# Neighbourhood attention: where the stacks of a head's second half and the second turn of V stand in the order of work

## The chip, the cores and the metric

The kernel runs on one core of a Trainium2 chip. The metric is the device time of one execution in microseconds (us); less is better. TensorE (PE) does the matrix products and the transposes, VectorE (DVE), ScalarE (ACT) and GpSimd (POOL) the element-wise work. Each engine works through its own list of instructions in order and waits at semaphores for the others.

## The reference, cut to what matters

Two post-LayerNorm layers on 1024 tokens of width 1024. The first mixes tokens by differential attention, the second, which the change is in, by attention over a neighbourhood of 8 rows by 16 columns on a grid of 16 rows by 64 columns. A gated feed-forward block with a short convolution follows each.

```python
def neighborhood_attention(x, w_qkv, b_qkv, rpb, w_o, b_o):
    qkv = x @ w_qkv + b_qkv                    # 16 heads of width 64
    ...
    def row(r):
        r_start = jnp.clip(r - kh // 2, 0, rows - kh)
        ...
        s = jnp.einsum('bchd,bicjhd->bhcij', q_row, k_sel)
        bias = rpb[:, row_off[None, :, None], col_off[:, None, :]]
        p = jax.nn.softmax((s + bias[None]).reshape(B, H, GRID_W, kh * kw), axis=-1)
        return jnp.einsum('bhcij,bicjhd->bchd', p, v_sel)
    ...
    return o @ w_o + b_o
```

## The kernel before

All matrix products are made in pieces: a float32 operand is split into a high part and the low remainder, and the products of high and low parts are added up in PSUM. Only `neighbourhood_stage` matters here. It takes the 16 heads in 8 pairs; a pair is `h` in the code and is called a head in this text. Each head has 16 steps `s`: steps 0 to 7 are the eight query tiles of its first half (`c` = 0), steps 8 to 15 those of its second half (`c` = 1). There are thus 128 steps, and the Python loops are unrolled: every engine has one long list, whose order is written out by hand.

In step `s` of head `h` the engines do this:

- **TensorE**: `score(h, s)` (into one of three PSUM banks), `turn` (four transposes of the probabilities of two steps back, into one of two banks `tb`), `weigh` (probabilities times V of four steps back, into `pb`), and then a chunk of the projection of the next head, `project(h + 1, j, ...)`. The six projection pieces `j` = 0 to 5 (two each for Q, K and V) have 24 matrix products each; `CHUNKS` deals them out as 12 in each of steps 0 to 3 and 8 in each later step. All six use the one PSUM bank `pa`, so that the first product of a piece waits until ScalarE has taken the piece before it out of `pa`.
- **VectorE**: adds the bias to the scores and takes the minimum (line 1841), makes the low part of the turned probabilities (`low`, line 1792), inverts the sum (line 1851), and every second step sums the output (`add_o`, lines 1806 and 1813).
- **ScalarE**: `high` (line 1725, the high part of the turned probabilities), the exponential (line 1770), `take_o` every second step (line 1740), and, where `TAKE` or the head's first line says so, `take(h, j)` (line 1716), which moves a finished projection piece from `pa` to `raw`.
- **GpSimd**: scales the probabilities (line 1516), splits weights, and builds the bias tables.

Each half of a head needs its **stacks**: the high parts of K and Q (`stacks` on ScalarE, lines 1748 and 1749), then the low parts and a copy (`stacks` on VectorE, lines 1819, 1822 and 1825), and a copy and the padded queries on GpSimd (`double_k`, `pad_q`). Steps 8 and on of the head need the stacks of the second half. They read `raw`, and `take(h + 1, 0)` in step 2, which overwrites `raw`, waits until VectorE has finished `stacks(h, 1)`'s reads:

```python
                        if TAKE[s] == 0:
                            act.wait_ge(stack_low[1], 2 * h + 2)
```

V of the head is turned in step 3 by `turn_v(h, 0)` and `turn_v(h, 1)`, four transposes each, into the same two banks `tb` that `turn` uses; each waits for the `low` that empties its bank. ScalarE's `high_v` (line 1732) and VectorE's `low_v` (line 1798) take the two halves out. The first `weigh` of the head, `weigh(h, 0)` in step 4, waits for both:

```python
                if s == 0:
                    pe.wait_ge(t_low, v_index(h, 1) + 1)
```

The list of ScalarE begins each head with `take(h, 5)`, the last piece of that head's own V; the first chunk of the next head's projection, in step 0, waits for it.

Of the kernel before, what the change touches and what calls it, by code (L numbers as in the profile page):

```python
# [1341 lines left out]
def neighbourhood_stage(nc, w_qkv, b_qkv, Z, OT, XTh, XTl, ident, S, GW, KH_, KW, shared_raw, next_tiles):  # L1342
# [3 lines left out]
    H = D // P  # L1346
# [20 lines left out]
    with ExitStack() as ctx:  # L1367
# [47 lines left out]
        def bank(h, j):  # L1415

            return pb[0] if h == 0 and j % 2 else pa

        def t_index(h, s):

            return TURNS * h + (s if s < 2 else s + 2)
# [9 lines left out]
        def back(h, s, n):  # L1431

            return (h, s - n) if s >= n else (h - 1, s - n + STEPS)
# [154 lines left out]
        def _(pe):  # L1588
# [92 lines left out]
            for h in range(H):  # L1681
                done = 0
                for s in range(STEPS):
                    score(h, s)
                    if h or s >= 2:
                        turn(*back(h, s, 2))
                    if h or s >= 4:
                        weigh(*back(h, s, 4))
                    if s == 3:
                        turn_v(h, 0)  # L1690
                        turn_v(h, 1)
                    if h + 1 < H:
                        project(h + 1, done // (3 * KT), done % (3 * KT), CHUNKS[s])
                        done += CHUNKS[s]
            for s in range(4):
                if s < 2:
                    turn(*back(H, s, 2))
                weigh(*back(H, s, 4))

        @block.scalar  # L1700
        def _(act):
            nc.scalar.preload_act_table(ACT.Exp)
            for j in range(3):

                if j == 2:
                    act.wait_ge(w_in[0], 16)
                nc.scalar.activation(wh[:, j], wraw[:, j % 2], ACT.Copy).then_inc(w_high, 1)
            act.wait_ge(b_turned, 1)
            nc.scalar.activation(bq[:].rearrange("p j h -> p (j h)"), pb[1][:, 0:3 * H], ACT.Copy).then_inc(b_set, 1)
            act.wait_ge(b_set, 1)  # L1710
            nc.scalar.activation(bq[:, 0], bq[:, 0], ACT.Copy, scale=-(DH ** -0.5)).then_inc(b_scaled, 1)
            act.wait_ge(b_scaled, 1)

            def take(h, j):
                act.wait_ge(proj_done, 6 * h + j + 1)
                nc.scalar.activation(raw[:, j // 2, (j % 2) * BANK:(j % 2 + 1) * BANK], bank(h, j)[:], ACT.Identity,  # L1716
                                     bias=bq[:, j // 2, h:h + 1],
                                     scale=-(DH ** -0.5) if j < 2 else 1.0).then_inc(proj_out, 1)

            def high(h, s):  # L1720
                step, i = STEPS * h + s, t_index(h, s)
                act.wait_ge(turned, i + 1)
                if step >= 3:
                    act.wait_ge(pv_done, step - 2)
                nc.scalar.activation(PT[:, step % 3, :, 0], tb[i % 2][:], ACT.Copy).then_inc(t_high, 1)

            def high_v(h, part):
                i = v_index(h, part)
                act.wait_ge(turned, i + 1)
                if h and part == 0:  # L1730
                    act.wait_ge(pv_done, STEPS * h)
                nc.scalar.activation(V[:, part * KB:(part + 1) * KB, :, 0],
                                     tb[i % 2][:].rearrange("p k (c d) -> p k c d", c=2), ACT.Copy).then_inc(t_high, 1)

            def take_o(h, s):
                pair = 8 * h + s // 2
                act.wait_ge(pv_done, STEPS * h + s + 1)
                if pair:
                    act.wait_ge(o_out, pair)
                nc.scalar.activation(otmp[:], pb[pair % 2][DH:P, :], ACT.Copy).then_inc(o_half, 1)  # L1740

            def stacks(h, c):
                a, _ = halves(c)
                if c == 0:
                    act.wait_ge(proj_out, 6 * h + 4)
                if h:
                    act.wait_ge(scored, STEPS * h - QT * (1 - c))
                nc.scalar.activation(KH[a, c], raw[a, 1], ACT.Copy).then_inc(stack_high[c], 1)
                nc.scalar.activation(QS[a, c], raw[a, 0], ACT.Copy).then_inc(stack_high[c], 1)

            for j in range(4):
                take(0, j)
            stacks(0, 0)
            take(0, 4)
            for h in range(H):
                take(h, 5)
                for s in range(STEPS):
                    step = STEPS * h + s
                    if s in TAKE and h + 1 < H:
                        if TAKE[s] == 0:  # L1760
                            act.wait_ge(stack_low[1], 2 * h + 2)
                        if TAKE[s] == 4:
                            act.wait_ge(turned, v_index(h, 1) + 1)
                        take(h + 1, TAKE[s])
                    if step >= 2:
                        high(*back(h, s, 2))
                    act.wait_ge(biased, step + 1)
                    if step >= 4:
                        act.wait_ge(turned, t_index(*back(h, s, 4)) + 1)
                    nc.scalar.activation(E[:, s % 4], Sc[step % 3][:], ACT.Exp, scale=-1.0, bias=mn[:, s % 4:s % 4 + 1],  # L1770
                                         accum_out=den[:, s % 4:s % 4 + 1]).then_inc(exped, 1)
                    if s % 2 and step >= 4:
                        take_o(*back(h, s, 4))
                    if s == 0:
                        stacks(h, 1)
                    if s == 3:
                        high_v(h, 0)
                        high_v(h, 1)
                    if s == 11 and h + 1 < H:
                        stacks(h + 1, 0)  # L1780
            for s in range(4):
                if s < 2:
                    high(*back(H, s, 2))
                if s % 2:
                    take_o(*back(H, s, 4))

        @block.vector
        def _(dve):
# [43 lines left out]
            for h in range(H):  # L1832
                for s in range(STEPS):
                    c, qt = s // QT, s % QT
# [3 lines left out]
                    if qt == 0:  # L1838
# [3 lines left out]
                                                   in1=bias.rearrange("p r k -> p (r k)"), scale=1.0, scalar=3.0e38,  # L1842
                                                   op0=ALU.add, op1=ALU.min,
                                                   accum_out=mn[:, s % 4:s % 4 + 1]).then_inc(biased, 1)
                    if step >= 2:
                        low(*back(h, s, 2))
                    if s == 3:
                        low_v(h, 0)
                        low_v(h, 1)
                    dve.wait_ge(exped, step + 1)  # L1850
                    nc.vector.reciprocal(rden[:, s % 4:s % 4 + 1], den[:, s % 4:s % 4 + 1]).then_inc(inverted, 1)  # L1851
                    if s % 2 and step >= 4:
                        add_o(*back(h, s, 4))
                    if s == 1:
                        stacks(h, 1)
                    if s == 12 and h + 1 < H:
                        stacks(h + 1, 0)
# [62 lines left out]
```

## Time and profile before

| | before |
|---|---|
| median of 3 runs | 2976.95 us (2975.7 to 2981.74) |
| profiled execution | 2978.02 us |
| its span in the profile | 2976.2 us |
| TensorE busy | 2764.6 us, 93% of the span |
| VectorE busy | 1801.3 us, 61% |
| ScalarE busy | 895.8 us, 30% |
| GpSimd busy | 1250.8 us, 42% |
| mean granted clock of TensorE | 0.974 of full speed |
| neighbourhood stage | about 1556 to 2102 us of the span |

The profiled execution lasted 1.82 us longer than its span and 1.07 us longer than the median. A share of busy time is a mean over stages. In the rows further down a number in square brackets behind an instruction is the time for which its engine sat idle right before it, and behind the arrow stands what ended that idle time.

### The profile page before, as it was taken

Reading aid. Unit: us, or ns where it says so; the run is one execution under the profiler, and the core shown is the slowest. Engines: PE = TensorE matmul, PEld = TensorE weight load, DVE = VectorE, ACT = ScalarE, POOL = GpSimd, SP = SyncE. Lnnn points to the kernel's source line nnn. Section 1 sums busy time; section 2 is a strip of 40 time slices with the busy share of each in tenths; the row PEclk is TensorE's granted clock in tenths of the full one; section 3 lists DMA queues with packets and bytes.
Section 4 is the critical chain, followed back from the end, with each engine's and each line's share of the span. In section 5 each row is a group of like instructions: output and inputs, shape, how many; then the busy total and the mean of one; then the engine's idle time right before and its main releaser. Section 6 shows DMA issues by size and latency. Waiting matters only on the chain. (4 is left out here: it accounts for less than half of the span.)

```text
span 2976.2 us, 36581 instructions
## 1 busy us (share of the span) xinstructions
PE 2764.6 (93%) x13387; PEld 2302.9 (77%) x13387; DVE 1801.3 (61%) x2190; ACT 895.8 (30%) x1314; POOL 1250.8 (42%) x890
## 2 busy tenths in 40 slices
PE   7999999968899999999979999998789999999998
PEld 6788888756778888887867887787667888888886
DVE  3666766654484555555573677767467554555557
ACT  3455445542311111111133555455322111111111
POOL 2444444233563333333444555555366333333335
PEclk9999999988999999999989999999899999999999
DMA  3000002215111111111121212111601111111111
GB/s 115 26 29 28 23 26 51 56 50 185 51 36 57 49 42 49 49 42 49 50 79 45 56 47 49 41 43 22 210 26 62 43 43 50 53 44 49 44 48 71
DMA packets 212649, 163.16 MB, mean 55 GB/s; under 512 B 34939, under 2 KB 194251, under 8 KB 212555
## 3 DMA queue, kind: packets, MB, share of 16 engines
q1 hardware_dynamic: 212411, 161.38, 18.4%
q8 instruction: 59, 0.97, 0.1%
q10 hardware_dynamic: 144, 0.52, 0.0%
q14 instruction: 35, 0.29, 0.0%
HBM read 137.24 MB, written 24.64 MB: 54 GB/s over the span
## 5 line engine op out<-in xcount | busy, mean ns | idle before, releaser
L1129 PE MATMUL ff_ph<-XTh,WH 128*128 128x512 f32 x1408 | 550.1, 391 | 6.8 <-PEq L41 6.8
L1129 PE MATMUL ff_ph<-XTl,WH 128*128 128x512 f32 x1408 | 549.3, 390 | 0.0
L1129 PE MATMUL ff_ph<-XTh,WL 128*128 128x512 f32 x1408 | 549.2, 390 | 0.0
L1067 POOL TENSOR_SCALAR WH<-raw_weights 128x1024 fp32r<-128x1024 f32 x128 | 153.5, 1200 | 846.6 <-PE ff_ph L1129 471.9
L1277 DVE TENSOR_SCALAR ff_C<-ff_H,ff_par 128x1024 f32<-128x1024 f32 x88 | 199.3, 2265 | 430.2 <-ACT ff_H L1225 429.5
L1069 POOL TENSOR_TENSOR WL<-raw_weights,WH 128x1024 fp32r<-128x1024 f32 x128 | 340.2, 2658 | 10.7
L1129 PEld LDWEIGHTS ff_ph<-XTh,WH 128*128 128x128 f32 x1408 | 265.4, 188 | 62.7 <-issue 7.6
L1129 PEld LDWEIGHTS ff_ph<-XTh,WL 128*128 128x128 f32 x1408 | 265.3, 188 | 55.4
L1129 PEld LDWEIGHTS ff_ph<-XTl,WH 128*128 128x128 f32 x1408 | 265.4, 189 | 55.1
L1225 ACT ACTIVATE ff_H<-ff_ph,ff_par 128x1024 f32<-128x1024 f32 x88 | 98.3, 1117 | 571.0 <-PE ff_ph L1129 571.0
L1270 DVE TENSOR_TENSOR X<-ff_po,X 128x512 f32<-128x512 f32 x288 | 192.1, 686 | 103.5 <-PE ff_po L1143 103.5
L1143 PE MATMUL ff_po<-WH 128*128 128x512 f32 x576 | 228.7, 397 | 23.0 <-DVE X L1270 20.7
L1143 PE MATMUL ff_po<-WL,WH 128*128 128x512 f32 x576 | 225.0, 391 | 0.0
L1143 PE MATMUL ff_po<-WH,WL 128*128 128x512 f32 x576 | 225.0, 391 | 0.0
L547 ACT ACTIVATE da_E<-da_S,da_mn 128x1024 f32<-128x1024 f32 x128 | 142.9, 1117 | 226.5 <-DVE da_mn L660 223.7
L1516 POOL TENSOR_SCALAR na_E<-na_E,na_rden 128x512 f32<-128x512 f32 x128 | 96.3, 753 | 213.3 <-DVE na_rden L1851 213.2
L1279 DVE SCALAR_TENSOR_TENSOR ff_C<-ff_H,ff_par,ff_C 128x1024 f32<-128x1024 f32 x88 | 168.9, 1919 | 11.0 <-DVE ff_C L1277 0.3
L1602 PE MATMUL na_pa<-XTh,na_wh 128*128 128x512 f32 x360 | 145.3, 404 | 28.9 <-ACT na_raw L1716 22.0
L347 PE MATMUL da_pa<-XTh,da_wh 128*128 128x512 f32 x360 | 151.5, 421 | 10.0 <-POOL da_wl L272 3.8
L278 POOL TENSOR_SCALAR da_E<-da_E,da_rden,da_neglam 128x1024 f32<-128x1024 f32 x64 | 76.6, 1197 | 199.8 <-DVE da_rden L674 199.8
L660 DVE CUSTOM_DVE_ANT_0 da_S<-da_S,da_strip 128x1024 f32<-128x1024 f32 x128 | 153.8, 1241 | 9.2 <-PE da_S L361 8.2
L1143 PEld LDWEIGHTS ff_po<-WH 128*128 128x128 f32 x576 | 108.4, 188 | 59.6 <-DVE X L1270 38.2
(222 smaller groups left out, 5952.0 us busy)
## 6 DMA issues: line engine op xcount, KB each, us to landing
raw_weights<-in_ffn_w_in SPq DMA_DIRECT2D x88, 512.0 KB, 3.8
raw_weights<-in_ffn_w_out SPq DMA_DIRECT2D x44, 512.0 KB, 3.5
raw_weights<-in_attn_w_qkv SPq DMA_DIRECT2D x24, 512.0 KB
raw_weights<-in_na_w_qkv SPq DMA_DIRECT2D x24, 512.0 KB, 4.2
wo_oraw<-heads_t SPq DMA_DIRECT2D x16, 512.0 KB, 4.7
rpb_rows<-da_rows SPq DMA_DIRECT2D x2, 3840.0 KB, 26.5
na_B<-rpb_rows SPq DMA_DIRECT2D x32, 224.0 KB, 4.2
da_E<-in_x SPq DMA_DIRECT2D x8, 512.0 KB, 5.7
```

Of the source, the lines that this page charges most:

```text
L347: last = nc.tensor.matmul(out[:], w[:, j // 2, k], x[:, k, t0:t0 + BANK], start=(i == 0), stop=(i == 3 * KT - 1))
L547: nc.scalar.activation(E[:, t % 2, c], Sc[c][:], ACT.Exp, scale=-1.0, bias=mn[:, t % 2, c:c + 1], accum_out=den[:, t % 2, c:c + 1]).then_i ...
L660: nc.vector.tensor_tensor_reduce(out=Sc[c][:], in0=Sc[c][:], in1=strip[:, (QT - 1 - t) * P:(QT - 1 - t) * P + S], scale=1.0, scalar=3.0e38 ...
L1067: nc.gpsimd.tensor_scalar(wh[:, slot], wraw[:, raw_slot], 1.0, 1.0, ALU.mult, ALU.mult).then_inc(w_high, 1)
L1069: nc.gpsimd.tensor_tensor(out=wl[:, slot], in0=wraw[:, raw_slot], in1=wh[:, slot].bitcast(F32), op=ALU.subtract).then_inc(w_low, 1)
L1129: last = nc.tensor.matmul(out[:, at], wt[:, slot, k * P:(k + 1) * P], x[:, k, at], start=(k == 0 and n == 0), stop=(k == KT - 1 and n == 2))
L1143: last = nc.tensor.matmul(po[r % 4][:], a[:, f, t * P:(t + 1) * P], wt[:, slots[f], half * BANK:(half + 1) * BANK], start=(f == 0 and n == ...
L1225: nc.scalar.activation(H[:, parity, 1:S + 1], ph[parity][:].rearrange("p k n -> p (k n)"), ACT.Identity, bias=par[:, 0, bass.ds(idx, 1)]). ...
L1270: nc.vector.tensor_tensor(out=at, in0=po[r % 4][:], in1=at, op=ALU.add).then_inc(added, 1)
L1277: nc.vector.tensor_scalar(c, h[:, 1:S + 1], tap[2], tap[4], ALU.mult, ALU.add).then_inc(conv_link, 1)
L1279: nc.vector.scalar_tensor_tensor(out=c, in0=h[:, 0:S], scalar=tap[1], in1=c, op0=ALU.mult, op1=ALU.add).then_inc(conv_link, 1)
L1602: last = nc.tensor.matmul(out[:], w[:, j // 2, k], x[:, k, t0:t0 + BANK], start=(i == 0), stop=(i == 3 * KT - 1))
```

## The change

Three edits of order; no instruction is added or removed, and what each computes is the same.

```diff
--- before.py
+++ after.py
@@ TensorE, step loop
                     if s == 3:
                         turn_v(h, 0)
-                        turn_v(h, 1)
                     if h + 1 < H:
                         project(h + 1, done // (3 * KT), done % (3 * KT), CHUNKS[s])
                         done += CHUNKS[s]
+                    if s == 3:
+                        turn_v(h, 1)
@@ ScalarE
-            stacks(0, 0)
+            for c in range(2):
+                stacks(0, c)
             take(0, 4)
             for h in range(H):
                 take(h, 5)
@@ ScalarE, step loop, behind take(h + 1, TAKE[s])
+                    if s == 4:
+                        high_v(h, 1)
                     if step >= 2:
                         high(*back(h, s, 2))
...
-                    if s == 0:
-                        stacks(h, 1)
                     if s == 3:
                         high_v(h, 0)
-                        high_v(h, 1)
                     if s == 11 and h + 1 < H:
                         stacks(h + 1, 0)
+                    if s == 15 and h + 1 < H:
+                        stacks(h + 1, 1)
@@ VectorE, step loop, behind the bias addition
+                    if s == 4:
+                        low_v(h, 1)
                     if step >= 2:
                         low(*back(h, s, 2))
                     if s == 3:
                         low_v(h, 0)
-                        low_v(h, 1)
...
-                    if s == 1:
+                    if s == 0:
                         stacks(h, 1)
```

**ScalarE, from step 15 of one head into step 2 of the next.** `na_E` is the exponential, `na_otmp` is `take_o`, `na_raw` is `take`, `na_PT` is `high`, and `na_KH` and `na_QS` are the stacks. Before:

```order
L1770 ACTIVATE na_E,na_den<-na_S,na_mn 128x512
L1740 ACTIVATE na_otmp<-na_pb 64x512
L1716 ACTIVATE na_raw<-na_pa,na_bq 128x512
L1725 ACTIVATE na_PT<-na_tb 128x4x128
L1770 ACTIVATE na_E,na_den<-na_S,na_mn 128x512
L1748 ACTIVATE na_KH<-na_raw 64x1024
L1749 ACTIVATE na_QS<-na_raw 64x1024
L1725 ACTIVATE na_PT<-na_tb 128x4x128
L1770 ACTIVATE na_E,na_den<-na_S,na_mn 128x512
L1740 ACTIVATE na_otmp<-na_pb 64x512
L1716 ACTIVATE na_raw<-na_pa,na_bq 128x512
```

The same stretch of the changed kernel, whose lines are numbered a little higher:

```order
L1774 ACTIVATE na_E,na_den<-na_S,na_mn 128x512
L1741 ACTIVATE na_otmp<-na_pb 64x512
L1749 ACTIVATE na_KH<-na_raw 64x1024
L1750 ACTIVATE na_QS<-na_raw 64x1024
L1717 ACTIVATE na_raw<-na_pa,na_bq 128x512
L1726 ACTIVATE na_PT<-na_tb 128x4x128
L1774 ACTIVATE na_E,na_den<-na_S,na_mn 128x512
L1726 ACTIVATE na_PT<-na_tb 128x4x128
L1774 ACTIVATE na_E,na_den<-na_S,na_mn 128x512
L1741 ACTIVATE na_otmp<-na_pb 64x512
L1717 ACTIVATE na_raw<-na_pa,na_bq 128x512
```

The two stacks have moved ahead of `take(h, 5)`, the first `na_raw`, and no longer stand between the exponential of step 0 and the `na_PT` of step 1.

**VectorE, step 4.** The bias addition is listed as two `ISA` rows, `na_PT` is `low`, `na_V` is `low_v`, `na_rden` the inversion. Before:

```order
L1813 TENSOR_TENSOR na_ostage<-na_osum 64x256
L1841 ISA na_S,na_mn<-na_S,na_BI 128x512
L1841 ISA na_mn 128x1
L1792 TENSOR_TENSOR na_PT<-na_tb,na_PT 128x4x128
L1851 RECIPROCAL na_rden<-na_den 128x1
```

The same stretch of the changed kernel:

```order
L1816 TENSOR_TENSOR na_ostage<-na_osum 64x256
L1844 ISA na_S,na_mn<-na_S,na_BI 128x512
L1844 ISA na_mn 128x1
L1801 TENSOR_TENSOR na_V<-na_tb,na_V 128x8x64
L1795 TENSOR_TENSOR na_PT<-na_tb,na_PT 128x4x128
L1855 RECIPROCAL na_rden<-na_den 128x1
```

V's second half now stands behind the bias addition of step 4, which itself waits for that step's scores.

**TensorE, the end of step 3 and step 4 up to the `weigh` that waits for V.** `na_pa` is the last product of step 3's chunk, `na_S` are the scores, `na_tb<-ident,na_E` is `turn`, `na_pb` is `weigh`, and `na_tb<-ident,na_raw` is `turn_v`. Before:

```order
L1602 MATMUL na_pa<-XTh,na_wl 128x512
L1622 MATMUL na_S<-na_KH,na_QS 128x448
L1623 MATMUL na_S<-na_KL,na_QS 128x448
L1628 MATMUL na_S<-na_KH,na_QZ 128x64
L1629 MATMUL na_S<-na_KL,na_QZ 128x64
L1628 MATMUL na_S<-na_KH,na_QZ 128x64
L1629 MATMUL na_S<-na_KL,na_QZ 128x64
L1638 MATMUL na_tb<-ident,na_E 128x128 x4
L1666 MATMUL na_pb<-na_PT,na_V 128x256 x4
```

The same stretch of the changed kernel:

```order
L1602 MATMUL na_pa<-XTh,na_wl 128x512
L1648 MATMUL na_tb<-ident,na_raw 128x128 x4
L1622 MATMUL na_S<-na_KH,na_QS 128x448
L1623 MATMUL na_S<-na_KL,na_QS 128x448
L1628 MATMUL na_S<-na_KH,na_QZ 128x64
L1629 MATMUL na_S<-na_KL,na_QZ 128x64
L1628 MATMUL na_S<-na_KH,na_QZ 128x64
L1629 MATMUL na_S<-na_KL,na_QZ 128x64
L1638 MATMUL na_tb<-ident,na_E 128x128 x4
L1666 MATMUL na_pb<-na_PT,na_V 128x256 x4
```

Before, the second four transposes of V stood with the first four, ahead of the twelve products of step 3; now only the scores and one `turn` lie between them and the `weigh` that needs their result. The lists of GpSimd and of the DMA queue are unchanged.

## Rows read from the trace of the kernel before

**Rows 1.** Who waited for whom on TensorE, 1556 to 2100 us (total, times, longest)
```profile
PE na_pa L1602 <- ACT na_raw L1716: 22.0, 14, 2.5
PE na_tb L1638 <- POOL na_E L1516: 13.0, 14, 2.2
PE na_tb L1648 <- DVE na_PT L1792: 9.3, 9, 4.8
```

**Rows 2.** Stretches: length, busy PE, PEld, DVE, ACT, POOL, granted clock, DMA
```profile
1595.00:1604.00 9.00, 7.77 (x38) 6.14 (x36) 4.79 (x9) 4.23 (x8) 3.50 (x3) 1.00 0.01 3
1604.00:1610.00 6.00, 5.33 (x19) 4.34 (x20) 2.81 (x5) 1.89 (x4) 2.43 (x3) 0.72 0.00 0
1722.00:1787.00 65.00, 60.84 (x354) 52.30 (x352) 45.98 (x89) 34.52 (x69) 35.76 (x37) 1.00 0.20 48
```

**Rows 3.** Timeline of ScalarE, end of the second head, start of the third
```profile
1723.22 0.60 ACT L1740 ACTIVATE na_otmp<-na_pb 64x512 f32<-64x512 f32 x1
1723.85 0.69 ACT L1716 ACTIVATE na_raw<-na_pa,na_bq 128x512 f32<-128x512 f32 x1
...
1726.17 0.69 ACT L1770 ACTIVATE na_E<-na_S,na_mn 128x512 f32<-128x512 f32 x1 [1.15 <-DVE na_mn L1841]
...
1726.97 1.05 ACT L1748 ACTIVATE na_KH<-na_raw 64x1024 fp32r<-64x1024 f32 x1
...
1729.00 0.60 ACT L1725 ACTIVATE na_PT<-na_tb 128x512 fp32r<-128x512 f32 x1
...
1735.33 0.69 ACT L1716 ACTIVATE na_raw<-na_pa,na_bq 128x512 f32<-128x512 f32 x1 [4.30 <-DVE na_QS L1822]
```

**Rows 4.** Timeline of TensorE, steps 0 to 4 of that head
```profile
1724.68 0.47 PE L1602 MATMUL na_pa<-XTh,na_wh 128*128 128x512 f32 x1 [0.91 <-ACT na_raw L1716]
...
1731.76 0.36 PE L1622 MATMUL na_S<-na_KH,na_QS 128*128 128x448 f32 x1
...
1736.07 0.50 PE L1602 MATMUL na_pa<-XTh,na_wh 128*128 128x512 f32 x1 [2.41 <-ACT na_raw L1716]
...
1740.68 0.60 PE L1648 MATMUL na_tb<-ident,na_raw 128*128 128x128 f32 x4
1741.78 0.66 PE L1648 MATMUL na_tb<-ident,na_raw 128*128 128x128 f32 x4 [0.50 <-DVE na_PT L1792]
1742.20 0.47 PE L1602 MATMUL na_pa<-XTh,na_wh 128*128 128x512 f32 x1
...
1745.05 0.36 PE L1622 MATMUL na_S<-na_KH,na_QS 128*128 128x448 f32 x1
...
1746.22 0.72 PE L1666 MATMUL na_pb<-na_PT,na_V 128*128 128x256 f32 x4
1746.78 0.39 PE L1602 MATMUL na_pa<-XTh,na_wh 128*128 128x512 f32 x1
```

**Rows 5.** Timeline of VectorE, steps 0 to 4 of that head
```profile
1726.98 0.16 DVE L1851 RECIPROCAL na_rden<-na_den 128x1 f32<-128x1 f32 x1 [0.30 <-ACT na_E L1770]
...
1732.82 1.22 DVE L1819 TENSOR_TENSOR na_KL<-na_raw,na_KH 64x1024 fp32r<-64x1024 f32 x1
...
1735.93 0.70 DVE L1841 CUSTOM_DVE_ANT_0 na_S<-na_S,na_BI 128x512 f32<-128x512 f32 x1
...
1736.55 0.69 DVE L1792 TENSOR_TENSOR na_PT<-na_tb,na_PT 128x512 fp32r<-128x512 f32 x1
...
1746.02 0.70 DVE L1841 CUSTOM_DVE_ANT_0 na_S<-na_S,na_BI 128x512 f32<-128x512 f32 x1 [0.65 <-PE na_S L1629]
```

**Rows 6.** Timeline of the first head, steps 1 to 3: VectorE, then TensorE
```profile
1601.04 1.22 DVE L1819 TENSOR_TENSOR na_KL<-na_raw,na_KH 64x1024 fp32r<-64x1024 f32 x1
...
1605.38 0.70 DVE L1841 CUSTOM_DVE_ANT_0 na_S<-na_S,na_BI 128x512 f32<-128x512 f32 x1
...
1604.67 0.50 PE L1602 MATMUL na_pa<-XTh,na_wh 128*128 128x512 f32 x1 [1.48 <-ACT na_raw L1716]
...
1609.11 0.37 PE L1622 MATMUL na_S<-na_KH,na_QS 128*128 128x448 f32 x1
```

## The prediction

> **What bounds the kernel now.** I read first the page's shares: TensorE is busy for 93% of the span, so a change outside the neighbourhood stage's TensorE list can matter only through its waits. The change is in that stage alone, so I asked next who was waited for on TensorE there. ScalarE's `take` costs it 22.0 us in 14 waits, GpSimd's scaling 13.0 us, VectorE's `low` in front of V's second turn 9.3 us [rows 1]. The stretch of one head, 65 us, has TensorE busy for 60.84 us at the full granted clock (1.00, 2.4 GHz), while VectorE, ScalarE and GpSimd are busy for 45.98, 34.52 and 35.76 us [rows 2]. So TensorE is the bound from head to head, and the time moves by what its four waits per head move. The timeline of one head shows them: 0.91 us at step 0 for `take(h, 5)`, 2.41 us at step 2 for `take(h + 1, 0)`, 0.50 us at step 3 for `low(h, 1)` [rows 4]; a fourth, for a scaling, isn't touched. The last head projects nothing and is bound by the smaller engines in turn.
>
> **The wait at step 2** is a chain over VectorE. Its stacks begin at 1732.82, behind the output sum of step 1 [rows 5]; ScalarE's `take(h + 1, 0)` has idled 4.30 us until K's and Q's low parts are made and starts at 1735.33 [rows 3]; TensorE follows at 1736.07 [rows 4]. In the changed kernel the stacks stand two output operations and one step earlier, so this wait should go.
>
> **The price at step 0.** `take(h, 5)` starts at 1723.85 with no idle time before it, right behind `take_o` of 1723.22 (0.60 us) [rows 3]: here ScalarE's own queue is the limit, and TensorE waits for it (0.91 us). The change puts both stacks of ScalarE between the two. They run from 1726.97 until the next instruction starts at 1729.00, 2.03 us [rows 3]. Nothing hides them: the projection can't start before `take` has emptied `pa`. So TensorE's first product of step 0 moves from 1724.68 to 1726.71, and its idle time grows to 2.94 us. That is the term which the change adds, and it is nearly as large as the one it removes.
>
> **Step 2, worked forward.** From the first product of step 0 to the scores of step 2 TensorE needs 1731.76 - 1724.68 = 7.08 us, so these start at 1733.79. From scores with four partial products to the next projection it needs 1746.78 - 1745.05 = 1.73 us [rows 4]; ready for step 2's chunk at 1733.79 + 1.73 = 1735.52. Is `take(h + 1, 0)` done by then? `take(h, 5)` now starts at 1725.88, `high` some 0.6 us later and takes as long, so that the exponential of step 0 starts at about 1727.06; the inversion follows 0.81 us behind it, at 1727.87, as that of 1726.98 [rows 5] follows the exponential of 1726.17 [rows 3]. VectorE's stacks begin at about 1728.05. They take 1735.93 - 1732.82 = 3.11 us in this head [rows 5], but 1605.38 - 1601.04 = 4.34 us in the first, where GpSimd's scaling begins beside them [rows 6]. In the new place it always does. The bias addition of step 1 thus starts at 1731.2 to 1732.4; 0.8 us to its exponential (it takes 0.70 us, and the minimum is read out behind it), 0.8 us through it, 0.6 us for `take_o`, and 0.75 us for `take` give 1734.1 to 1735.3, and never before the previous chunk's end, 1733.8, plus 0.75. All of it lies before 1735.52. So the wait is gone, and the chunk starts 0.55 us before its old time of 1736.07. It holds by 0.2 us at the upper bound.
>
> The Trainium skill (GPSIMD Engine Reference, section 8, Key points) says that GpSimd shares its SBUF interfaces with VectorE and contends with two-input operations. The pair 3.11 and 4.34 us agrees with it; it gives no figure for this pair.
>
> **Step 3.** The first turn of V moves with the chunk: 1740.68 - 0.55 = 1740.13. Before, chunk three began 1742.20 - 1740.68 = 1.52 us behind it; one turn alone passes in 1742.20 - 1741.78 = 0.42 us. The chunk starts at 1740.55, takes 1745.05 - 1742.20 = 2.85 us, the second turn starts at 1743.40, the scores of step 4 at 1743.82 [rows 4]. Two turns now cost 0.84 us instead of 1.52, a gain of 0.68; the idle 0.50 understates it.
>
> **A new wait at step 4.** `weigh(h, 0)` needs `low_v(h, 1)`, and VectorE has this behind the bias addition of step 4, which waits for step 4's scores. That addition starts 1746.02 - 1745.05 = 0.97 us behind the scores' start [rows 4, 5]. The next operation ends 1736.55 + 0.69 - 1735.93 = 1.31 us behind the addition's start [rows 5]. With 0.05 us to TensorE, as from `take`'s end (1736.02) to 1736.07, `weigh` starts at 1743.82 + 0.97 + 1.31 + 0.05 = 1746.15; without the wait it would be 1743.82 + 1.17 = 1744.99. So 1.16 us are lost, where before there was no wait. ScalarE's `high_v(h, 1)` is not late: the turn ends at 1744.06 and `take(h + 1, 1)` lies beside it. Late next behind `low_v` is `low` of step 2, which has until step 6.
>
> **The sum.** Per head +2.03 - 2.58 - 0.68 + 1.16 = -0.07 us: `weigh(h, 0)` at 1746.15 instead of 1746.22. Behind it the list is the old one. Six heads have all four terms (the second to the seventh): -0.4 us. The first has no step-0 term, since its stacks run on ScalarE during the opening projections. Its VectorE stacks start some 3.7 us earlier, and its wait of 1.48 us [rows 6] shrinks to about 0.3, so -1.2; V's two terms are about -1.0 and +1.16. Together -1.0 to -1.4. In the last head nothing is projected: the stacks leave VectorE's step 1 for step 0, the bias addition of step 2 still ends where the same total work ends, and V's two `low_v` change places with an addition; I take +0.3, bounds -0.5 and +1.5. Sum: -0.4 - 1.2 + 0.3 = -1.3 us. From the profiled execution's 2978.02 us (1.82 above its span) that is 2976.7; the median of the runs shown is 1.07 us lower, so 2975.6 us. Within 0.2% (6 us), about what a measurement of this kernel can tell from no change.
>
> **Rivals.** (1) The clock falls in the longer stall: slower. In the first head the granted clock is 0.72 from 1604 to 1610, after a stretch with waits of which the last is 1.48 us [rows 2, 6]: twelve products take 1609.11 - 1604.67 = 4.44 us instead of 2.85, a loss of 1.59. Against it: the third head keeps 1.00 through a wait of 2.41 us [rows 2, 4], and no wait of the later heads for `take` is longer than 2.5 [rows 1]. But 2.94 us is longer than any of these, and the quiet stretch begins with short transposes. The mechanism: step 0's stall lets the clock fall to 1.2 GHz for the chunk behind it, in each of six heads. Price 6 x 1.59 = 9.5, total 2975.6 + 9.5 = 2985.1 us; from five heads on it decides for slower. In one to three heads it gives 2977 to 2980, still no change. The Trainium skill (TensorE: Matmul & The Clock Gate, Part 1) says the clock is gated by how busy the array has lately been, only between half and full rate. The 0.72 is a mixture of these two; by that rule the longer stall is the riskier. (2) The wait at step 2 stays in part, because VectorE's stacks with GpSimd beside them hold up step 1: for 1 us more than my upper bound, +0.8 per head and 2981, for 1.2 us and more slower than by 0.2%, up to 2984. Against it stand the bounds above. (3) The new wait at step 4 doesn't appear, VectorE getting to `low_v` before the bias addition's scores are needed: -1.16 in seven heads, 2967.5. Against it stands the order of VectorE's list. (4) ScalarE's stacks are hidden at step 0, and the change does what its parts promise: six times 2.03 less, 2963. Against it: `take(h, 5)` without idle time.
>
> **How the numbers follow.** My sum within 0.2%: 0.50. Rival 1 in few heads, also no change: 0.14; in five or six: 0.17. Rival 2 beyond 0.2%: 0.06. Rival 3: 0.08; rival 4: 0.03; 0.02 for a last head worse than its bound. Faster 0.11, same 0.64, slower 0.25. An error of 0.4 us per head in the four terms is 2.4 us, with the last head's bounds some 3 us either way; the range reaches down towards rival 3 and up to rival 1: 2970.5 to 2985.5.
>
> **What would show it.** Right: per head a wait of about 2.9 us at step 0 for line 1717, none at step 2, none before either turn of V, and about 0.9 us of idle time before step 4's `weigh`, released by VectorE's `low_v`; head to head 64.85 us instead of 64.92. Wrong: granted clock under 1.00 in the heads' stretches (rival 1), a wait at step 2 for `take` (rival 2), no idle before that `weigh` (rival 3), a step-0 wait still near 0.9 us (rival 4).

## The result, and the profile after

The changed kernel takes 2985.20 us (median of 9 runs, 2983.76 to 2987.50) against 2978.56 us (9 runs, 2975.70 to 2981.74) for the kernel before, timed beside it: a ratio of 1.0023, 95% interval 1.0013 to 1.0033. It is slower by 0.23%. The forecast was 2975.6 us and no change; the first rival, the clock that falls in the longer stall, gave 2985.1 us and slower.

The profiled execution took 2984.45 us, with a span of 2982.6 us against 2976.2 us before. The page of the changed kernel, its span and the busy time of each engine:

```profile
span 2982.6 us, 36581 instructions
PE 2774.4 (93%) x13387; PEld 2310.5 (77%) x13387; DVE 1805.3 (61%) x2190; ACT 893.5 (30%) x1314; POOL 1252.8 (42%) x890
```

This says nothing of the cause yet. The waits on TensorE in the neighbourhood stage do. The view that answers to [rows 1], for the changed kernel (total us, times, longest):

```profile
PE na_pa L1602 <- ACT na_raw L1717: 18.0, 7, 2.9
PE na_tb L1638 <- POOL na_E L1516: 15.7, 15, 3.5
PE na_pb L1666 <- DVE na_V L1801: 7.4, 8, 1.1
...
PE na_tb L1648 <- DVE na_PT L1795: 1.2, 2, 0.7
```

`take` was waited for 14 times, at most 2.5 us; now there are 7 waits, and six of them are of 2.93 to 2.94 us, all at step 0. The nine waits before V's turns are two, and both lie in the last head. A wait for `low_v` (line 1801) is new, eight times. For `take` and V together TensorE waits 18.0 + 7.4 + 1.2 = 26.6 us where it waited 22.0 + 9.3 = 31.3; with the scalings (15.7 instead of 13.0) it is 42.3 instead of 44.3. By its waits the kernel should be a little faster.

What it gave back is in the stretches. Each row below is one head of the changed kernel (the third and the fourth), from one step-0 wait to the next; the columns are those of [rows 2], the granted clock third from the end:

```profile
1719.10:1785.40 66.30, 62.05 (x353) 53.37 (x352) 46.33 (x91) 34.23 (x68) 36.46 (x37) 0.97 0.20 47
1785.40:1852.60 67.20, 63.04 (x352) 54.15 (x352) 46.23 (x91) 34.23 (x68) 36.33 (x37) 0.95 0.19 46
```

TensorE has the 352 products that it had, but is busy for 62 to 63 us with them instead of 60.84 [rows 2], and the granted clock is 0.97 or 0.95 instead of 1.00. The timeline of TensorE for steps 0 to 4 of the third head, which answers to [rows 4], shows where:

```profile
1723.58 0.67 PE L1602 MATMUL na_pa<-XTh,na_wh 128*128 128x512 f32 x1 [2.94 <-ACT na_raw L1717]
1724.05 0.63 PE L1602 MATMUL na_pa<-XTl,na_wh 128*128 128x512 f32 x1
1724.48 0.63 PE L1602 MATMUL na_pa<-XTh,na_wl 128*128 128x512 f32 x1
...
1727.54 0.39 PE L1602 MATMUL na_pa<-XTl,na_wh 128*128 128x512 f32 x1
1727.76 0.39 PE L1602 MATMUL na_pa<-XTh,na_wl 128*128 128x512 f32 x1
1727.99 0.39 PE L1622 MATMUL na_S<-na_KH,na_QS 128*128 128x512 f32 x1
...
1732.21 0.36 PE L1622 MATMUL na_S<-na_KH,na_QS 128*128 128x448 f32 x1
...
1733.95 0.39 PE L1602 MATMUL na_pa<-XTh,na_wh 128*128 128x512 f32 x1
...
1738.43 0.60 PE L1648 MATMUL na_tb<-ident,na_raw 128*128 128x128 f32 x4
1738.79 0.48 PE L1602 MATMUL na_pa<-XTh,na_wh 128*128 128x512 f32 x1
...
1741.63 0.60 PE L1648 MATMUL na_tb<-ident,na_raw 128*128 128x128 f32 x4
1741.99 0.45 PE L1622 MATMUL na_S<-na_KH,na_QS 128*128 128x448 f32 x1
...
1744.41 0.74 PE L1666 MATMUL na_pb<-na_PT,na_V 128*128 128x256 f32 x4 [0.91 <-DVE na_V L1801]
```

Behind the wait of 2.94 us the products follow each other at 0.43 us (1724.05 to 1724.48), at the end of the same chunk at 0.22 us (1727.54 to 1727.76). That is 1.2 and 2.4 GHz. The chunk takes 1727.99 - 1723.58 = 4.41 us. From there to step 4 there is no wait, at step 2 and before either turn of V, and then the 0.91 us before `weigh`.

The lengths of heads in this text are measured on TensorE from the `turn` of one head's step 0 (behind its 0.34 us wait for a scaling) to that of the next; the first head begins with the stage's first product and the last ends with the first product of the next stage. The six later heads (second to seventh) take 399.02 us in the changed kernel and 389.50 before: 66.50 instead of 64.92 us each, +9.52 us. The first head takes 2.99 us less, the last one 2.16 us more. Together +8.69 us for the stage (562.23 instead of 553.54). The rest of the span, which the change doesn't touch, came out 2.3 us shorter in this profile. That is noise of this size: in the eleven profiles of this case the part ahead of the stage alone, which no edit touches, took between 1557.8 and 1562.7 us, and the 9 runs of the kernel before lie 6 us apart. So a single profile's stage and a median agree only to a few microseconds.

### The profile page after: what moved, and what is told of

Its sections match the earlier page's. It is cut to its first block and busy times, and to the rows that moved or that the text cites. A ratio compares the mean times of both kernels' runs of the same rounds, so it can differ in the third digit from the quotient of the medians.

```text
span 2982.6 us, 36581 instructions
## 1 busy us (share of the span) xinstructions
PE 2774.4 (93%) x13387; PEld 2310.5 (77%) x13387; DVE 1805.3 (61%) x2190; ACT 893.5 (30%) x1314; POOL 1252.8 (42%) x890
## 5 line engine op out<-in xcount | busy, mean ns | idle before, releaser
L1516 POOL TENSOR_SCALAR na_E<-na_E,na_rden 128x512 f32<-128x512 f32 x128 | 103.1, 805 | 239.1 <-DVE na_rden L1855 239.1
```

The lines of the kernel that those rows point to most:

```text
L1516: nc.gpsimd.tensor_scalar(E[:, b], E[:, b], rden[:, b:b + 1], 1.0, ALU.mult, ALU.mult).then_inc(scaled, 1)
```

## The experiments

Nine kernels, each timed against the kernel before. The runs were made on three chips (e1_fill, e2_stacks, e3_v and e5_behind on one, e6_best, e7_half, e8_v_fill and e9_bstacks on another, e10_before_fill on a third), so the column "before" shows what the kernel before took beside each, and medians of different chips compare less exactly than their differences from it. Two theories stand against each other. By the first the loss is the clock that falls behind the step-0 wait, and the order alone costs nothing. By the second it is in the order itself, above all in the `weigh` that waits for V, and the clock is only a sign of idle time.

| kernel | median us (runs) | before, us | ratio, 95% interval |
|---|---|---|---|
| e1_fill | 2973.45 (11) | 2979.74 | 0.9979, 0.9970 to 0.9988 |
| e2_stacks | 2980.49 (11) | 2979.74 | 1.0006, 0.9997 to 1.0015 |
| e3_v | 2989.93 (7) | 2979.74 | 1.0034, 1.0022 to 1.0045 |
| e5_behind | 2971.29 (8) | 2979.74 | 0.9972, 0.9961 to 0.9982 |
| e7_half | 2976.81 (11) | 2978.83 | 0.9990, 0.9981 to 0.9999 |
| e8_v_fill | 2982.36 (11) | 2978.83 | 1.0011, 1.0002 to 1.0020 |
| e9_bstacks | 2961.26 (5) | 2978.83 | 0.9941, 0.9928 to 0.9955 |
| e6_best | 2956.27 (5) | 2978.83 | 0.9925, 0.9912 to 0.9939 |
| e10_before_fill | 2976.11 (11) | 2979.49 | 0.9986, 0.9977 to 0.9995 |

**The changed kernel with products in the step-0 wait (e1_fill).** The order of all instructions is that of the changed kernel. In heads two to seven, TensorE does twelve products more while it would wait. They go into a bank of scores that is free then and is overwritten later, so the output is unchanged.

```diff
                     if s == 3:
                         turn_v(h, 0)
+                    if s == 0 and h and h + 1 < H:
+                        pe.wait_ge(exped, STEPS * h - 1)
+                        for i in range(12):
+                            nc.tensor.matmul(Sc[(STEPS * h + 1) % 3][:], wh[:, 2, i % KT], XTh[:, i % KT, 0:BANK],
+                                             start=True, stop=True)
                     if h + 1 < H:
```

> The changed kernel with twelve further matrix products on TensorE in step 0 of the second to seventh head, put between the weigh and the projection, where it otherwise idles 2.94 us for take(h, 5). They write a score bank that the next step overwrites, so the output is unchanged; at the full clock they take some 2.7 us, less than the wait. Theory (the clock falls because of the quiet stretch): the granted clock stays 1.00 in these six heads, a head takes 64.9 us instead of 66.5, and the kernel is 9.5 us faster than the changed one, about 2975.7, 1 to 3 us below the kernel before. Rival (the chunk behind the stall is slow for another reason, such as ScalarE's or GpSimd's traffic beside it): the twelve products of the chunk still take 4.4 us, and the time stays at 2985.

It took 2973.45 us, 11.7 us less than the changed kernel's 2985.20 and 6.3 less than the kernel before beside it, with more work for the bounding engine. The expectation had 1 to 3 us below the kernel before. The stretch of the third head, in e1_fill:

```profile
1719.00:1783.70 64.70, 63.32 (x365) 54.36 (x365) 45.94 (x89) 34.53 (x69) 36.41 (x36) 1.00 0.20 48
```

And the timeline of TensorE at step 0 of that head, in e1_fill:

```profile
1720.02 2.98 PE L1694 MATMUL na_S<-XTh,na_wh 128*128 128x512 f32 x12
1723.13 0.47 PE L1602 MATMUL na_pa<-XTh,na_wh 128*128 128x512 f32 x1
1723.44 0.39 PE L1602 MATMUL na_pa<-XTl,na_wh 128*128 128x512 f32 x1
1723.67 0.40 PE L1602 MATMUL na_pa<-XTh,na_wl 128*128 128x512 f32 x1
```

The chunk's products now follow at 0.23 us from the start, and the clock is 1.00 in every head; the wait before `weigh` is still there in all of them. The six heads take 64.63 to 64.69 us, 1.85 us less than in the changed kernel, 11.07 us for the six (387.95 instead of 399.02). The order is the same and only the wait was filled, so the loss is in the clock behind that wait, as the first theory has it. Of the 6.3 us below the kernel before, the profiles show only 2.0 in the stage (551.53 instead of 553.54 us); where the rest arises is open. The profiled run of the kernel before (2978.02 us) is one of its faster ones: beside e1_fill its runs went from 2975.37 to 2983.19 us, with a mean granted clock of 0.975 in the first and 0.970 in the last.

**Each half of the change alone (e2_stacks, e3_v).** e2_stacks moves only the stacks, and V is turned as before; e3_v moves only V's second turn and leaves the stacks. As differences from the changed kernel:

```diff
# e2_stacks
                     if s == 3:
                         turn_v(h, 0)
+                        turn_v(h, 1)
...
-                    if s == 3:
-                        turn_v(h, 1)
# e3_v, ScalarE and VectorE
+                    if s == 0:
+                        stacks(h, 1)
...
-                    if s == 15 and h + 1 < H:
-                        stacks(h + 1, 1)
...
-                    if s == 0:
+                    if s == 1:
                         stacks(h, 1)
```

> The kernel before with only the stacks moved (ScalarE step 15, VectorE step 0); V as before. Theory: a wait of 2.94 us at step 0 and none at step 2, -0.55 us per head from the order of work, and a fall of the clock worth +1.6 us per head in six heads; the first head gains 1.4 to 3 us; in sum +2 to +5 us against the kernel before, 2981 to 2984. Rival (the clock falls only with V's turn moved too, or by chance of the run): the clock stays 1.00 and the kernel is 4 to 6 us faster than before.

> The kernel before with only V's second turn moved behind step 3's chunk. Theory: -0.68 us for the turn, +1.16 us for the weigh of step 4, so +0.48 us in each of seven heads, and +1 to +3 us in the last head, where no chunk hides anything: +4 to +6 us, 2983. The wait at step 2 stays 2.41 us and the clock stays at 1.00 in the later heads. Rival (the last head's loss comes from the stacks): only +3.4 us, and the last head takes as long as before.

e2_stacks: 2980.49 us, just under the expected range, and a change from the kernel before that the interval doesn't tell from none. The step-0 wait of 2.94 us and the falls behind it are there in all six heads, as expected, which are 65.6 to 67.0 us long, together 7.27 us more than before. The first head is 3.23 us shorter, the last 0.20 us longer: +4.2 us for the stage of this profile, where the medians lie 0.75 us apart.

e3_v was a miss: +10 us where +4 to +6 were expected. The waits of this kernel for `take` are those of before:

```profile
PE na_pa L1602 <- ACT na_raw L1717: 22.1, 14, 2.5
...
PE na_pb L1666 <- DVE na_V L1800: 7.4, 8, 1.1
```

but its stretches are not. Two heads in a row, the second and the third, in e3_v:

```profile
1659.30:1726.20 66.90, 62.28 (x352) 53.45 (x352) 45.67 (x89) 34.46 (x69) 35.63 (x36) 0.97 0.19 46
1726.20:1791.50 65.30, 60.72 (x352) 52.30 (x352) 45.63 (x89) 34.44 (x69) 35.60 (x36) 1.00 0.20 47
```

The clock falls in five of six heads although the longest wait is the 2.44 to 2.46 us that it stood through in all six heads of the profile before. In the first head it is the other way round: behind the same wait of 1.48 us the clock fell in the profile before [rows 2, 6] and holds in e3_v. TensorE at step 2 of the second and of the third head, in e3_v:

```profile
1672.84 0.50 PE L1602 MATMUL na_pa<-XTh,na_wh 128*128 128x512 f32 x1 [2.46 <-ACT na_raw L1717]
...
1674.39 0.63 PE L1602 MATMUL na_pa<-XTl,na_wh 128*128 128x512 f32 x1
1674.81 0.63 PE L1602 MATMUL na_pa<-XTh,na_wl 128*128 128x512 f32 x1
...
1739.71 0.50 PE L1602 MATMUL na_pa<-XTh,na_wh 128*128 128x512 f32 x1 [2.44 <-ACT na_raw L1717]
...
1741.43 0.39 PE L1602 MATMUL na_pa<-XTl,na_wh 128*128 128x512 f32 x1
1741.66 0.39 PE L1602 MATMUL na_pa<-XTh,na_wl 128*128 128x512 f32 x1
```

The same instructions behind the same wait run at 0.43 us apart in one head and at 0.23 us in the next. Without the fall a head is 65.3 us, 0.4 us above 64.92: this is what V's new place costs by its order, and the last head is 1.56 us longer. This much agrees with the expectation; the rest should be clock, which the next run tests.

**Products in e3_v's wait, and in that of the kernel before (e8_v_fill, e10_before_fill).** If that last sentence holds, ten products in front of step 2's chunk must give it back in e3_v, and next to nothing in the kernel before. The edit is the same in both:

```diff
+                    if s == 2 and h + 1 < H:
+                        pe.wait_ge(exped, STEPS * h + 1)
+                        for i in range(10):
+                            nc.tensor.matmul(Sc[(STEPS * h + 3) % 3][:], wh[:, 2, i % KT], XTh[:, i % KT, 0:BANK],
+                                             start=True, stop=True)
```

> The kernel with only V's second turn moved (e3_v), with ten further products into a free score bank at step 2, in the wait for take(h + 1, 0) of 2.4 us. In e3_v the clock fell behind this wait in most heads, in the kernel before, with the same wait, in the first head alone. Theory (it is the quiet stretch at step 2): no fall in any head, a head takes 65.4 us or a little less, and the kernel is 7 to 9 us faster than e3_v, 2981 to 2983. Rival (V's later turn is what slows the array): the falls and 2990 stay.

> Control: the kernel before with ten further products into a free score bank at step 2, in the wait for take(h + 1, 0) of 2.41 us (1.48 us in the first head, where they cost up to 0.8 us). Theory (the fillers act through the clock alone): the first head's chunk takes 2.85 us instead of 4.44, the other heads stay at 64.9 us or 0.2 below it, and the time is 0 to 3 us less than before. Rival (fillers speed a head by something else, which would also explain their effect on the changed kernel): heads faster by 1 us or more although the clock was 1.00 there without them, 2970 or less.

e8_v_fill took 2982.36 us, 7.6 us less than e3_v (6.7 by the differences from the kernel before on each chip), with no fall in the six heads (65.32 to 65.37 us each, 8.7 us less for the six). e10_before_fill took 2976.11 us, 3.4 us less than the kernel before, a little more than expected. Its later heads are as long as they were, 64.83 to 64.90 us; most of its 2.1 us within the stage is the first head's, where the clock was 0.72 [rows 2] and is now, in the same stretch:

```profile
1604.00:1610.00 6.00, 6.00 (x33) 5.14 (x33) 3.81 (x7) 1.95 (x4) 2.99 (x3) 1.00 0.00 0
```

So the products of themselves bring next to nothing where no clock is lost (0.3 us over six heads). That they gain in e1_fill isn't an effect of the products as such.

**The step-0 wait made shorter (e5_behind, e7_half).** In e5_behind ScalarE makes both stacks right behind `take(h, 5)` instead of ahead of it. In e7_half K's stack stays ahead and Q's goes behind.

```diff
# e5_behind
                 take(h, 5)
+                stacks(h, 1)
...
-                    if s == 15 and h + 1 < H:
-                        stacks(h + 1, 1)
# e7_half
                 take(h, 5)
+                if h:
+                    stacks(h, 1, "q")
...
-                        stacks(h + 1, 1)
+                        stacks(h + 1, 1, "k")
```

> The changed kernel with ScalarE's two stacks right behind take(h, 5) instead of ahead of it, all else as changed. Theory: the wait at step 0 is 0.91 us again, the clock holds 1.00, and a wait of some 0.9 us comes back at step 2, because TensorE is there 2.03 us earlier than take(h + 1, 0): -1.5 us at step 2 and +0.48 us for V per head against the kernel before. About 2973 to 2976 with the last head's loss. Rival (the clock falls for another reason than the length of step 0's wait): clock under 1.00 in the heads and 2980 or more.

> The changed kernel with only K's stack ahead of take(h, 5), and Q's right behind it. The wait at step 0 becomes 1.9 us instead of 2.94 or 0.91. Theory (the longer the wait the more often the clock falls): the clock holds in most heads, so 1.0 us less per head from the wait and up to 1.6 from the clock: 2971 to 2977. Rival (any wait much over 0.9 us lets it fall, as the first head's 1.48 us did before): clock falls in most heads, 2978 to 2982.

e5_behind took 2971.29 us, somewhat below what was expected. Its clock is 1.00 in all heads, which are 63.94 us long; the wait at step 0 is 0.91 us again, and one of 1.01 us is left at step 2. In e7_half the step-0 wait is 1.98 to 1.99 us in each of six heads, and the clock falls in four of them. TensorE at step 0 of the second and of the third head, in e7_half:

```profile
1656.73 0.47 PE L1602 MATMUL na_pa<-XTh,na_wh 128*128 128x512 f32 x1 [1.98 <-ACT na_raw L1717]
...
1659.57 0.39 PE L1622 MATMUL na_S<-na_KH,na_QS 128*128 128x512 f32 x1
...
1720.80 0.76 PE L1602 MATMUL na_pa<-XTh,na_wh 128*128 128x512 f32 x1 [1.99 <-ACT na_raw L1717]
...
1724.99 0.39 PE L1622 MATMUL na_S<-na_KH,na_QS 128*128 128x512 f32 x1
```

2.84 us for the twelve products in one and 4.19 in the other. With 2976.81 us it lies between e5_behind and the changed kernel, inside the expected 2971 to 2977; but the expectation had the clock hold in most heads, and it fell in most, as its rival said.

**A better order (e6_best, e9_bstacks).** e6_best keeps the thought of the change and takes away its prices: ScalarE's stacks stand behind `take(h, 5)`, VectorE's right behind the bias addition of step 0, ahead of `low` and the inversion, and V's second turn stands inside step 3's chunk, behind its third product, with `high_v` and `low_v` where the kernel before has them. e9_bstacks has the same stacks and leaves V as before.

```diff
# e6_best, TensorE
+                        n = 3 if s == 3 else CHUNKS[s]
+                        project(h + 1, done // (3 * KT), done % (3 * KT), n)
+                        done += n
                     if s == 3:
                         turn_v(h, 1)
+                        if h + 1 < H:
+                            project(h + 1, done // (3 * KT), done % (3 * KT), CHUNKS[s] - 3)
+                            done += CHUNKS[s] - 3
# both, VectorE, behind the bias addition
+                    if s == 0:
+                        stacks(h, 1)
                     if step >= 2:
                         low(*back(h, s, 2))
```

> A version meant to beat both: ScalarE's stacks of the second half right behind take(h, 5), VectorE's right behind the bias addition of step 0 (ahead of low and the inversion), V's second turn inside step 3's chunk behind its third product, and V's high and low parts where they were before. Theory: the wait at step 0 stays 0.91 us, the one at step 2 shrinks from 2.41 us to 0 to 0.5, no wait at either turn of V nor at step 4's weigh, clock 1.00 in all heads: 1.9 to 2.4 us and 0.68 us less per head in seven heads, 2958 to 2963. Rival (VectorE's queue then holds up low and the inversion, so that turn and weigh of step 2 wait instead): a wait at step 2 of 1 us or more for another cause, 2968 or more.

> The same stacks as in e6_best, with V untouched from the kernel before. Theory: as there without the 0.68 us per head, 2963 to 2967; the difference to e6_best is the price of V's second turn in its old place. Rival (V's old wait is hidden once the rest is earlier): no difference between the two.

e6_best took 2956.27 us, 0.75% less than the kernel before, and e9_bstacks 2961.26 us; both are just below what was expected. TensorE at steps 0, 2 and 3 of the third head, in e6_best:

```profile
1718.63 0.47 PE L1602 MATMUL na_pa<-XTh,na_wh 128*128 128x512 f32 x1 [0.91 <-ACT na_raw L1721]
...
1728.28 0.50 PE L1602 MATMUL na_pa<-XTh,na_wh 128*128 128x512 f32 x1 [0.67 <-ACT na_raw L1721]
...
1732.89 0.60 PE L1648 MATMUL na_tb<-ident,na_raw 128*128 128x128 f32 x4
...
1734.03 0.62 PE L1648 MATMUL na_tb<-ident,na_raw 128*128 128x128 f32 x4
```

Heads are 62.48 us, with a clock of 1.00: 0.67 to 0.70 us remain of the 2.41 at step 2, and neither turn of V waits, nor does the `weigh` of step 4. In e9_bstacks heads are 63.16 us and the 0.50 us before V's second turn is back. The difference, 0.68 us per head, is just what the prediction gave for taking the two turns apart; in all it is 5.0 us. e9_bstacks against e5_behind is VectorE's place for the stacks and V's old place in one, 10.0 us together (9.1 by the differences from the kernel before on each chip), and was not taken apart.

## Why the prediction was wrong

**The wait at step 0: right.** 2.94 us was worked out, 2.93 to 2.94 is there in all six heads. ScalarE's timeline in the changed kernel, which answers to [rows 3], is the one that was worked out, with the stacks from 1720.73 until `take(h, 5)` starts at 1722.75, 2.02 us later (2.03 predicted):

```profile
1720.73 1.05 ACT L1749 ACTIVATE na_KH<-na_raw 64x1024 fp32r<-64x1024 f32 x1
...
1722.75 0.69 ACT L1717 ACTIVATE na_raw<-na_pa,na_bq 128x512 f32<-128x512 f32 x1
...
1732.47 0.69 ACT L1717 ACTIVATE na_raw<-na_pa,na_bq 128x512 f32<-128x512 f32 x1 [1.50 <-PE na_pa L1602]
```

Rival 4, that this is hidden, is out.

**No wait at step 2: right.** The last row has turned round: `take(h + 1, 0)` idled 4.30 us for VectorE [rows 3] and now idles 1.50 us for TensorE. The chunk starts 1733.95 - 1732.21 = 1.74 us behind the scores (1.73 predicted). VectorE in the changed kernel, which answers to [rows 5]:

```profile
1724.82 1.22 DVE L1822 TENSOR_TENSOR na_KL<-na_raw,na_KH 64x1024 fp32r<-64x1024 f32 x1
1726.07 1.60 DVE L1825 TENSOR_TENSOR na_QS<-na_raw,na_QS 64x1024 fp32r<-64x1024 f32 x1
1727.60 0.68 DVE L1828 CAST na_KL<-na_KL 64x1024 fp32r<-64x1024 f32 x1
...
1743.05 0.70 DVE L1844 CUSTOM_DVE_ANT_0 na_S<-na_S,na_BI 128x512 f32<-128x512 f32 x1 [0.53 <-PE na_S L1629]
...
1743.67 0.69 DVE L1801 TENSOR_TENSOR na_V<-na_tb,na_V 128x512 fp32r<-128x512 f32 x1
```

The three stacks take 1727.60 + 0.68 - 1724.82 = 3.46 us, between the bounds of 3.11 and 4.34. Part of that ease was bought by the slower chunk, which gave VectorE 1.56 us more; but in e1_fill, where the clock holds, the stage has a single wait for `take`, of 0.4 us, in step 0 of the first head. Rival 2 is out.

**V's turns and the new wait: right.** A turn costs 1738.79 - 1738.43 = 0.36 us where it doesn't wait (0.42 predicted), `weigh` starts 1744.41 - 1741.99 = 2.42 us behind the scores (2.33 predicted), held by `low_v`, which stands behind the bias addition. Rival 3 is out.

**The sum of the order, -0.07 us per head: right in its sense.** e1_fill, where the clock holds, has 64.65 us per head against 64.92, -0.27 us. The excess of 0.2 us, 1.2 us over six heads, is partly the cheaper turns (twice 0.06); the rest was not traced.

**What failed is the choice between the sum and rival 1.** The sum had no term for the clock: it let TensorE run at 1.00 behind the longer wait, and gave rival 1 in five or six heads 0.17, because the clock held through 2.41 us in every later head and 2.94 us is only half a microsecond more. It fell in six heads of six, and the term is +11.1 us. e1_fill shows that it decides the sign: the same order with the clock held is faster than the kernel before, by 6.3 us in the medians and 2.0 us in the stage of the profiles. What the prediction rested on, six heads of equal length in one profile, bore little: in e3_v the clock fell in five of six heads behind the same wait. Its row on the other side, 0.72 behind a wait of 1.48 us in the first head, was no firmer, since e3_v holds the clock there. The Trainium skill (TensorE: Matmul & The Clock Gate, Part 1) has the clock at full rate or at half of it; the two product pitches of the trace, 0.43 and 0.22 us, agree with it. By the same part a block sets the rate by how busy the array has lately been; that fits e1_fill, where products in the wait kept the rate, but no run here shows what that block measures.

**The price of a fall, 1.59 us, was sized too small.** It was taken from one chunk of the first head. From step 0's first product to step 1's, e7_half's second head takes 1660.99 - 1656.73 = 4.26 us without a fall, and the six heads of e1_fill 4.22 to 4.27. The changed kernel's six heads take 5.83, 5.83, 6.82, 5.76, 6.72 and 5.67 us: the falls cost 1.4 to 2.6 us, 11.1 us in sum, and not 9.5. In the fourth and sixth heads all twelve products run at the lower clock, and in the others six to eight. TensorE in the fourth head of the changed kernel, the first product of the chunk and the scores behind its twelfth, 5.25 us later:

```profile
1789.80 0.76 PE L1602 MATMUL na_pa<-XTh,na_wh 128*128 128x512 f32 x1 [2.94 <-ACT na_raw L1717]
...
1795.05 0.54 PE L1622 MATMUL na_S<-na_KH,na_QS 128*128 128x512 f32 x1
```

Less the 11.1 us, the changed kernel's six heads are 387.9 us, 64.65 each: just those of e1_fill. That closes the account for them: -1.6 us by order, +11.1 us by clock, +9.5 us in all. That rival 1's 2985.1 us met the measured 2985.2 is partly luck. It stands 8.2 us above its base, 2976.95 us (a median of 3 runs); the measured difference is 6.6 us, from 2978.56 (9 runs). And its price of the falls was too small, while what the order gives was too small on the other side.

**The first head, -1.0 to -1.4 us, was sized too small.** It is -2.99 us. At step 2 the wait of 1.48 us is gone altogether, where 0.3 us was to remain, and the clock no longer falls there: its chunk takes 2.85 us, which gives back the 1.59 us that the prediction itself had read from [rows 6]; -1.4 us is left for the order. The prediction used this fall as the price of a rival and did not ask whether the change would take it away. That the vanished wait is what kept the clock is likely, not shown: in e3_v it held there with the wait of 1.48 us in place.

**The last head, +0.3 us with bounds -0.5 and +1.5, was sized too small.** It is +2.16 us. e2_stacks has +0.20 us there and e3_v +1.56 us, so V's term is the larger one. The stretch of the last head with the 12.4 us of idle time behind it, in the kernel before and in the changed one:

```profile
2047.20:2112.80 65.60, 36.52 (x232) 32.40 (x232) 42.25 (x96) 36.72 (x72) 21.88 (x28) 0.82 0.21 60
2052.20:2120.00 67.80, 39.51 (x232) 34.41 (x232) 43.99 (x96) 36.41 (x72) 22.50 (x28) 0.77 0.20 58
```

TensorE is busy for 39.5 of 67.8 us, with the 232 products that took 36.5 us before, and the granted clock is 0.77 instead of 0.82. The lower clock alone doesn't lengthen this head much: in e2_stacks it is 0.77 too, with 38.5 us busy, for +0.20 us. The `weigh` of step 4 waits 1.09 us for `low_v` there too, and the scores of the step after it stand behind it in TensorE's list; with no chunk between them the smaller engines wait for these scores in turn. That they do is argued from the order; no run takes this wait alone out of the last head.

## What to carry to other kernels

Work put ahead of the instruction that frees the bounding engine's buffer was paid in full here, and paid twice: the longer stall costs its own length and the lower clock behind it. In this kernel the second was the larger (11.1 us, where the order alone gained). So before moving work into such a stall look for the place right behind the freeing instruction, where the same stacks brought 8.4 us instead of losing 6.6. Where a stall can't be shortened, independent products in it held the clock (8.7 and 11.1 us over six heads), and brought next to nothing where no clock was lost. That a wait kept the clock in every head of one profile is weak evidence: the same wait lost it in five of six heads of e3_v. And the first and last heads, where other things bound, want a sum of their own.

## What the runs showed of the hardware

- No length of wait separates the falls from the rest. In the heads after the first the clock fell behind 2.94 us in six of six (changed kernel, e2_stacks), behind 2.41 to 2.46 us in none of six before and in five of six in e3_v, behind 1.98 to 1.99 us in four of six (e7_half), and never behind waits of 0.91 to 1.17 us (e5_behind, first head included). In the first head it fell behind a wait of 1.48 us in the kernel before and held behind the same wait in e3_v. Each count is of one profiled execution. In e7_half and e3_v the same instructions behind the same wait did both, one head after the other. What decides between them is open: it wasn't tried to shift a head in time and leave all else as it is.
- The fall needn't begin with the wait's end. In the second head of the changed kernel the first six products behind the wait follow at 0.23 us and the next ones at 0.43; in e3_v it is the first one or two in the second head and the first five in the fourth.
- VectorE's stack of 64x1024 with two inputs took 1.22 us, 1.60 us and, in the third head of e6_best (its timeline of VectorE), 2.65 us:

```profile
1720.13 2.65 DVE L1823 TENSOR_TENSOR na_KL<-na_raw,na_KH 64x1024 fp32r<-64x1024 f32 x1
```

The Trainium skill (GPSIMD Engine Reference, section 8, Key points) names contention between GpSimd and VectorE operations with two SBUF inputs; beside the 2.65 us GpSimd ran its low part of the weights (line 1491, 1719.24 to 1721.69 us), which reads two inputs too. GpSimd can be the slower one instead: in the changed kernel's third head the stack of 1.22 us (from 1724.82) had a scaling beside it (from 1724.88) that took 1.72 us, where one with no stack beside it took 0.70 us in the kernel before (from 1730.69). But no run here took GpSimd's work away from beside the stacks, so that it is the cause of the 1.4 us isn't shown. e6_best gained in spite of it.
